# Last pair of experts: a third quarter of the down weights as whole rows, the context rows' residual through TensorE, and one fp32 pass for the last 256 columns

## The reference

```python
a = jnp.einsum('becd,edf->becf', xs, w_gate)
u = jnp.einsum('becd,edf->becf', xs, w_up)
y = jnp.einsum('becf,efd->becd', jax.nn.silu(a) * u, w_down)
y = y * gate[..., None].astype(y.dtype)
# the slots are added back to their tokens; then x = x + g2 * that
```

## Time and profile before

| | |
|---|---|
| median of 3 runs | 1518.87 us (1518.62 to 1519.34) |
| the profiled execution's own time | 1518.44 us |
| its span, first to last instruction | 1516.8 us |
| TensorE busy | 1447.9 us, 95% |
| VectorE, ScalarE busy | 623.8 us and 255.1 us |
| HBM read and written | 565.02 MB and 6.55 MB |
| mean granted TensorE clock | 0.987 of full speed |

### The profile page before, as it was taken

How to read it: one execution, slowest core, us unless ns; L and a number is a source line. 1 busy time by engine, 2 the same in 40 slices (tenths; PEclk the granted TensorE clock), 3 DMA queues, 4 the chain that set the end, 5 groups by cost and what they waited for, 6 DMA issues and landing times.

```text
span 1516.8 us, 18489 instructions
## 1 busy us (share of the span) xinstructions
PE 1447.9 (95%) x7806; PEld 883.1 (58%) x7806; DVE 623.8 (41%) x1033; ACT 255.1 (17%) x358; POOL 26.7 (2%) x58
## 2 busy tenths in 40 slices
PE   6999999999999999999999999999999889999998
PEld 3667799888899997445435335335335335335433
DVE  4454977877799996101301301301301301211313
ACT  4233223333234323000000000000000000000200
POOL 0000000000000000000000000000000000000000
PEclk8999999999999999999999999999999999999999
DMA  9999698777778759999999999999999999999999
GB/s 375 402 395 366 252 331 294 278 259 261 274 275 292 253 175 382 396 434 432 430 432 430 432 431 434 430 432 431 433 431 430 433 433 431 430 430 430 434 420 355
DMA packets 99855, 572.48 MB, mean 377 GB/s; under 512 B 9612, under 2 KB 54612, under 8 KB 76756
## 3 DMA queue, kind: packets, MB, share of 16 engines
q1 hardware_dynamic: 88416, 520.14, 84.0%
q0 software_dynamic: 6912, 50.33, 8.7%
q10 hardware_dynamic: 4468, 1.14, 0.3%
HBM read 565.02 MB, written 6.55 MB: 377 GB/s over the span
## 4 chain that ended last, share of the span: by engine, by line
PE 73%; DMA 20%; DVE 3%; SPq 2%; issue 1%; ACT 1%; DVEq 0%; ACTq 0%
PE psum L653 71%; DMA ring<-in_w_up 18%; SPq L563 2%; DMA ring<-in_w_ada 1%; DMA ring<-in_w_down 1%; SPq L450 1%; DVE w_parts L1541 1%; PE psum L663 1%; DVE ring L1689 0%; PE psum L852 0%; PE psum L1108 0%; PE psum L1078 0%; ACT w_parts L1241 0%; DVE mix L1826 0%; PE psum L815 0%
## 5 line engine op out<-in xcount | busy, mean ns | idle before, releaser
L653 PE MATMUL psum<-ring,hid 128*64 128x512 f32 x3024 | 685.9, 601 | 45.9 <-DMA ring<-in_w_up 32.6
L653 PEld LDWEIGHTS psum<-ring,hid 128*64 128x64 f32 x3024 | 243.7, 139 | 464.6 <-issue 415.5
L2004 DVE TENSOR_TENSOR hid<-psum,hid 128x512 f32<-128x512 f32 x16 | 11.1, 692 | 514.9 <-PE psum L653 514.9
L653 PE MATMUL psum<-h_parts,w_parts 128*128 128x384 f32 x1152 | 207.0, 337 | 0.0
L653 PEld LDWEIGHTS psum<-h_parts,w_parts 128*128 128x128 f32 x1152 | 199.9, 188 | 3.5 <-issue 2.5
L1541 DVE TENSOR_TENSOR w_parts<-ring,w_parts 128x2048 fp32r<-128x2048 f32 x52 | 118.9, 2287 | 48.5 <-ACT w_parts L1241 48.2
L1241 ACT ACTIVATE w_parts<-ring 128x2048 fp32r<-128x2048 f32 x52 | 99.6, 1915 | 195.3 <-PE psum L653 164.3
L653 PE MATMUL psum<-w_parts,h_parts 128*128 128x512 f32 x432 | 103.3, 395 | 0.6 <-DVE h_parts L1585 0.6
L653 PE MATMUL psum<-ring,early 128*32 128x512 f32 (+6 forms) x654 | 92.8, 538 | 7.5 <-DMA ring<-in_w_ada 6.3
L653 PEld LDWEIGHTS psum<-w_parts,h_parts 128*128 128x128 f32 x432 | 79.7, 188 | 25.6 <-issue 9.2
L653 PEld LDWEIGHTS psum<-early,mix 128*128 128x128 f32 x768 | 86.6, 192 | 9.0 <-issue 9.0
(11 more groups left out here) (223 smaller groups left out, 771.4 us busy)
## 6 DMA issues: line engine op xcount, KB each, us to landing
ring<-in_w_up SPq DMA_DIRECT2D x30, 4096.0 KB, 22.7
ring<-in_w_gate SPq DMA_DIRECT2D x28, 4096.0 KB, 29.3
ring<-in_w_down SPq DMA_DIRECT2D x26, 4096.0 KB, 29.4
ring<-in_w_ada POOLq DMA_DIRECT2D x48, 1024.0 KB, 6.9
ring<-in_w_in SPq DMA_DIRECT2D x36, 1024.0 KB, 8.3
ring<-in_w_ada SPq DMA_DIRECT2D x28, 768.0 KB, 15.6
res<-in_w_ada SPq DMA_DIRECT2D x16, 1024.0 KB, 7.0
ring<-in_w_out SPq DMA_DIRECT2D x16, 1024.0 KB, 5.7
```

Source lines behind the costliest of these rows:

```text
L653: return nc.tensor.matmul(out, lhsT, rhs, start=start, stop=stop, skip_group_check=True)
L2004: tt(by_row, bank[1][:, :].rearrange("p (b a) -> p a b", a=4), by_row, ALU.mult).then_inc(act_ready, 1)
```

## The change

Three things change, all in the last pair.

1. `FULL` goes from 2 to 3: the first two of the four rows of the second part also come as whole rows, as four loads of 1 MB in the double slot that q = 6 left. Only the last two rows come by column blocks, ten loads, all in the double slot that q = 7 left. TensorE has a third `down_full`, and each `down_tail` has half the rows. `TAIL_ORDER` has no split block.
2. The residual of the context tile is copied by ScalarE as fp32r (`kept_hi`), and VectorE makes its rest (`kept_lo`), both before the first block. `send_last` puts two passes with the identity matrix ahead of the context tile's passes, ScalarE copies the finished tile out of PSUM (`ctx_result`), and VectorE no longer adds it. VectorE also copies the identity matrix to `ident_r`.
3. The last block of 256 columns isn't split into two fp32r parts: its sending reads `y_all` in fp32. ScalarE's copy and VectorE's `y_rest` are left out for it.

```diff
-FULL = 2
+FULL = 3
-TAIL_ORDER = [("d", 0), ("h", 1), ("s", 0), ("r", 1), ("d", 2), ("s", 1), ("d", 3), ("s", 2), ("d", 4), ("s", 3), ("s", 4)]
+TAIL_ORDER = [("d", 0), ("d", 1), ("s", 0), ("d", 2), ("s", 1), ("d", 3), ("s", 2), ("d", 4), ("s", 3), ("s", 4)]
...
+        kept_hi = parts_at("kept_hi", D, res_at)
+        kept_lo = parts_at("kept_lo", D, hid_at)
+        ident_r = parts_at("ident_r", P, early_at + 4 * BANK)
...
             def full_load(n, jj, e):
-                sp.dma_start(full_rows(n, e)[:, jj, :], down_pairs(e, 0, n)[:, jj, :]).then_inc(full_landed[2 * n + jj], 16)
+                sp.dma_start(full_rows(n, e)[:, jj, :], down_pairs(e, n // 2, n % 2)[:, jj, :]).then_inc(full_landed[2 * n + jj], 16)
-            def tail_load(b, half, e):
+            def tail_load(b, e):
                 col, width = TAIL[b]
-                sp.dma_start(tail_slot(b, e)[:, 2 * half:2 * half + 2, :], down_pairs(e, 1, half)[:, :, col:col + width])\
-                    .then_inc(tail_landed[b][half], 16)
+                sp.dma_start(tail_slot(b, e), down_pairs(e, 1, 1)[:, :, col:col + width]).then_inc(tail_landed[b], 16)
...
+            sp.wait_ge(moe_used, LAST + WIDE + FULL + 1)
             for b in range(len(TAIL)):
-                sp.wait_ge(moe_used, LAST + WIDE + FULL + TAIL[b][0] // 1024 + 1)
-                for half in range(2):
-                    for e in range(2):
-                        tail_load(b, half, e)
+                for e in range(2):
+                    tail_load(b, e)
...
-                sp.wait_ge(last_out, NT * b + 1)
+                sp.wait_ge(ctx_out, b + 1)
-                sp.wait_ge(last_out, NT * (b + 1))
+                sp.wait_ge(last_out, (NT - 1) * (b + 1))
...
-            def down_tail(b, rows=range(4)):
+            def down_tail(b):
                 width = TAIL[b][1]
-                for jj in rows:
-                    if jj % 2 == 0:
-                        pe.wait_ge(tail_landed[b][jj // 2], 32)
+                pe.wait_ge(tail_landed[b], 32)
+                for jj in range(2):
...
             def send_last(b):
                 first, width = TAIL[b]
-                pe.wait_ge(y_last, b + 1)
+                cols = slice(first, first + width)
                 for t in range(NT):
                     n = NT * b + t
                     if SENDS[n] in SENDS[:n]:
-                        pe.wait_ge(last_out, n - SENDS[:n][::-1].index(SENDS[n]))
+                        old = n - 1 - SENDS[:n][::-1].index(SENDS[n])
+                        if old % NT == 0:
+                            pe.wait_ge(ctx_out, old // NT + 1)
+                        else:
+                            pe.wait_ge(last_out, (NT - 1) * (old // NT) + old % NT)
...
-                    mm(out, rows, y_hi[:, first:first + width], True, False)
-                    mm(out, rows, y_lo[:, first:first + width], False, True).then_inc(sent, 1)
+                    if t == 0:
+                        pe.wait_ge(kept_parts, 4)
+                        mm(out, ident_r[:, :], kept_hi[:, cols], True, False)
+                        mm(out, ident_r[:, :], kept_lo[:, cols], False, False)
+                    if b == len(TAIL) - 1:
+                        pe.wait_ge(tail_y, b + 1)
+                        mm(out, rows.bitcast(F32), y_all[:, cols], t > 0, True).then_inc(sent, 1)
+                    else:
+                        pe.wait_ge(y_last, b + 1)
+                        mm(out, rows, y_hi[:, cols], t > 0, False)
+                        mm(out, rows, y_lo[:, cols], False, True).then_inc(sent, 1)
...
+            for n in range(0, len(ROW_SENDS), NT):
+                cols = slice(ROW_SENDS[n][0] * BLK, (ROW_SENDS[n][0] + 1) * BLK)
+                a.wait_ge(row_added, n + 1)
+                copy(kept_hi[:, cols], y_rows[:, 0, cols]).then_inc(kept, 1)
+
+            def ctx_result(b):
+                first, width = TAIL[b]
+                a.wait_ge(sent, 16 * (PAIRS - 2) + NT * b + 1)
+                copy(y_rows[:, 0, first:first + width], bank[SENDS[NT * b]][:, 0:width]).then_inc(ctx_out, 1)
+
             for b, (first, width) in enumerate(TAIL):
-                a.wait_ge(tail_y, b + 1)
-                copy(y_hi[:, first:first + width], y_all[:, first:first + width]).then_inc(tail_hi, 1)
+                if b < len(TAIL) - 1:
+                    a.wait_ge(tail_y, b + 1)
+                    copy(y_hi[:, first:first + width], y_all[:, first:first + width]).then_inc(tail_hi, 1)
+                if b:
+                    ctx_result(b - 1)
+            ctx_result(len(TAIL) - 1)
...
             copy(actT, bank[4][:, :]).then_inc(actT_ready, 1)
+            copy(ident_r[:, :], ident[:, :])
             product(PAIRS - 1, 1, 8)
...
             add_rows(range(ROWS_LATE, len(ROW_SENDS)))
+            for n in range(0, len(ROW_SENDS), NT):
+                cols = slice(ROW_SENDS[n][0] * BLK, (ROW_SENDS[n][0] + 1) * BLK)
+                v.wait_ge(kept, n // NT + 1)
+                tt(kept_lo[:, cols], y_rows[:, 0, cols], kept_hi[:, cols].bitcast(F32), ALU.subtract).then_inc(kept_parts, 1)
...
             for b in range(len(TAIL)):
                 y_scale(b)
                 if b:
-                    result(b - 1, range(0, 1))
-                y_rest(b)
+                    result(b - 1, range(1, 2))
+                if b < len(TAIL) - 1:
+                    y_rest(b)
                 if b:
-                    result(b - 1, range(1, NT))
-            result(len(TAIL) - 1, range(NT))
+                    result(b - 1, range(2, NT))
+            result(len(TAIL) - 1, range(1, NT))
```

More of the change, by code:

```diff
@@ L163, in build @@
         ring = sb("ring", [P, RING, SLOT])
+        res_at = here()
         res = sb("res", [P, KC * T])
@@ L267, in build @@
         add_rows_of = sb("add_rows_of", [P, 33])
+        early_at = here()
         early = sb("early", [P, 32 * KC + KC * NE + P + 256])
@@ L350, in build @@
         moe_landed = [sem(f"moe_landed{n}") for n in range(WIDE)]
-        tail_landed = [[sem(f"tail_landed{n}_{half}") for half in range(2)] for n in range(len(TAIL))]
+        tail_landed = [sem(f"tail_landed{n}") for n in range(len(TAIL))]
         full_landed = [sem(f"full_landed{n}") for n in range(2 * FULL)]
@@ L384, in build @@
         tail_y, tail_hi = sem("tail_y"), sem("tail_hi")
+        kept, kept_parts, ctx_out = sem("kept"), sem("kept_parts"), sem("ctx_out")
         y_scaled, row_sent, row_added = sem("y_scaled"), sem("row_sent"), sem("row_added")
@@ L416, in tail_slot @@
             first, width = TAIL[b]
-            at = 8 * first + 4 * width * e
-            flat = ring[:, WIDE_AT[FULL + first // 1024]:WIDE_AT[FULL + first // 1024] + 2, :].rearrange("p s n -> p (s n)")
-            return flat[:, at % (2 * SLOT):at % (2 * SLOT) + 4 * width].rearrange("p (j n) -> p j n", j=4)
+            at = 4 * first + 2 * width * e
+            flat = ring[:, WIDE_AT[FULL]:WIDE_AT[FULL] + 2, :].rearrange("p s n -> p (s n)")
+            return flat[:, at:at + 2 * width].rearrange("p (j n) -> p j n", j=2)
         class Chain:
@@ L1062, in down_full @@
                                full_rows(n, e)[:, jj, col:col + width], n == 0 and jj == 0, False)
-            def down_tail(b, rows=range(4)):
+            def down_tail(b):
                 width = TAIL[b][1]
-                for jj in rows:
-                    if jj % 2 == 0:
-                        pe.wait_ge(tail_landed[b][jj // 2], 32)
+                pe.wait_ge(tail_landed[b], 32)
+                for jj in range(2):
                     for e in range(2):
                         last = mm(bank[TAIL_BANKS[b]][ES * e:ES * e + ES, 0:width], tail_rows(e, 2 * FULL + jj),
-                                  tail_slot(b, e)[:, jj, :], False, jj == 3)
+                                  tail_slot(b, e)[:, jj, :], False, jj == 1)
                 return last
@@ L1229, in _ @@
                     send_last(b)
-                elif what == "h":
-                    down_tail(b, range(0, 2))
                 else:
-                    down_tail(b, range(2, 4) if what == "r" else range(4)).then_inc(moe_used, 1)
+                    down_tail(b).then_inc(moe_used, 1)
         @block.scalar
```

## The result

The changed kernel takes 1521.63 us (median of 21 runs, 1520.46 to 1522.94) against 1519.09 us (21 runs, 1518.05 to 1520.05) of the kernel before in the same comparison: ratio 1.0016, 95% interval 1.0011 to 1.0022. That is 2.4 us slower by the ratio (2.5 by the medians), clear of noise, and within 0.2%, though the interval reaches just beyond. The forecast was 2.2 us slower: 1521.1 us, in a range of 1519.0 to 1522.9, with 0.70 for within 0.2%.

What follows compares the result with a forecast made beforehand. Loading paces the kernel up to its last weight, then TensorE's remaining work sets the end. From the last whole row at 1495.7 its terms sum to 19.9 us; the end moves 2.2 us, median 1521.1 us, range 1519.0 to 1522.9.

Steps and rivals of the forecast that it cites:

- The landings: Last pair's loads: new whole-row pairs in at 1490.7 and 1495.7, at 421 GB/s; block 1 in at 1501.1.
- TensorE unbroken behind the last whole row: Last pair: TensorE's products and sendings after 1495.7 take 19.9 us, with 0.2 us waiting, no rest from 1501.1 on.
- the sum: TensorE's steps from the last whole row at 1495.7: 19.9 us to last issue, VectorE's last result at 1516.25.
- the fp32 pass: Last 256-column block's sending: 0.43 us a tile, 1.29 for three against 0.70 for six fp32r passes, +0.59.
- the second whole row: TensorE's product with the second new row pair, for all five blocks: 3.44 us, from 1495.7 to 1499.2.
- block 4's two passes with the change of operand: Last block's sending: 0.23 us for the residual's two passes plus 0.1 for a change of kind of operand.
- The waits: TensorE before the two new whole rows: about 1.4 us (1489.3 to 1490.7) and 1.5 us.
- The rival itself: TensorE's clock falls in the new waits, if one reaches some 2.2 us: 1.7 us slower, 1522.8; chance 0.13.
- whole rows land no faster: Rival on the new loads: last whole row 0.9 us later, no faster than 2 KB pieces, 1522.0; chance 0.08.
- the extra passes are hidden: Rival on the sendings: the 1.85 + 0.59 us don't show, 1518.9 to 1520; chance 0.13.
- What it takes from VectorE: Residual in the last stretch: five VectorE results of about 0.35 to 0.68 us, said to be hidden already.
- the residual's net price: Two more TensorE passes in each of five blocks' sendings: 1.85 us on the path.

Runs made afterwards that it cites:

- rows in pieces: Changed kernel with the four new whole-row loads cut into pieces of 512 columns (2 KB); 1522.47 us against 1519.25 for the kernel before, ratio 1.0022.
- residual alone: Kernel before plus only the residual by TensorE and ScalarE; loads, order and last block unchanged; 1520.25 us against 1519.38, ratio 1.0006.
- whole rows alone: Kernel before plus only the third quarter's whole rows and their block order; 1521.31 us against 1519.38, ratio 1.0011.
- short results: Kernel before plus whole rows and their block order, context tile's results cut to 8 columns per block; 1521.36 us against 1519.25, ratio 1.0011.
- scale sooner: Kernel before plus whole rows, context results cut to 8 columns, scales of blocks 3 and 4 each ahead of one result; 1521.18 us against 1519.58, ratio 1.0011.
- sends late: Kernel before plus fp32 pass, block 1 sent before block 2's second half, blocks 2 to 4 after all products; 1519.60 us against 1519.25, ratio 1.0004.

## Why the prediction was right, point by point

**The landings.** Forecast 4.9, 9.9 and 15.3 us behind the point; measured 4.96, 9.94 and 15.37. The pace of whole rows, read from issue and landing times of two pairs of loads, held to 0.2% here (9.96 and 9.94 us) and to 1% in three other profiles (10.02 to 10.05). The working starts that landing at 1485.7 where the earlier trace rows has 1485.80, so its absolute times are 0.1 us early.

**TensorE unbroken behind the last whole row.** From there to VectorE's last result the sum gave 20.55 us; it was 1516.94 - 1496.38 = 20.56. Most terms came out within 0.02 us (2.04 and 1.87, 1.02, 1.05 and 0.43 a tile), the fp32 pass by the scaling with columns from 384. Two did not and made up for each other: the second whole row took 3.50 us, not 3.44, since it starts behind a wait, and block 4's two passes with the change of operand took 0.25 us (1514.77 to 1515.02), not 0.23 + 0.1. The mechanism held; that the sum came out to 0.01 us is in part luck. That the landings move the end was shown by the rows in pieces: 0.90 us later in, 0.90 us later out.

**Faster transfer, later end.** The whole rows did what they were meant to: the third quarter lands 0.90 us sooner than in pieces. Yet they cost 1.28 us in the changed kernel. By TensorE's sum that is because a whole row goes to all five blocks and none can be finished and sent until the last of them is in.

**The waits.** Forecast 1.4 and 1.5 from product to product; measured 1.47 and 1.48 (1.76 and 1.78 in the weight loads' rows). The granted clock stayed at 1.00. In the rows in pieces the two were 2.22 us in the weight loads' rows, and the sum above held to 0.01 us there too, so the clock cost nothing. The earlier trace rows counts by the products' rows; there the new waits are 1.31 and 1.32 us and those of the rows in pieces 1.76, so no run took this stage to the 2.20 after which the clock had fallen.

The rival itself was misread. It took 1.70 us for the longest wait without a fall and some 2.2 us for the length that decides. But the same trace has longer ones without a fall, and the changed kernel more of them (the first two rows are before, the others changed):

```profile
842.79 8.78 PE L653 MATMUL psum<-ring,hid 128*64 128x512 f32 x32 [2.53 <-DMA ring<-in_w_up]
...
1250.76 7.09 PE L653 MATMUL psum<-ring,hid 128*64 128x512 f32 x32 [2.63 <-DMA ring<-in_w_up]
843.27 8.74 PE L659 MATMUL psum<-ring,hid 128*64 128x512 f32 x32 [2.54 <-DMA ring<-in_w_up]
...
1134.70 7.09 PE L659 MATMUL psum<-ring,hid 128*64 128x512 f32 x32 [2.63 <-DMA ring<-in_w_up]
```

Of 11 such waits of 2.20 to 2.66 us, 8 were followed by slow products before and 4 in the changed kernel. A wait of this length alone doesn't say whether the clock falls.

**The rivals.** That whole rows land no faster was refuted by 421 against 387 GB/s. That the extra passes are hidden was refuted by the unbroken row of TensorE, and by residual alone (+1.05, of which 0.92 are passes).

**What was wrong in it.** One step of the residual's part: "What it takes from VectorE [...] was hidden [...] and in the last stretch it follows TensorE." That holds for the kernel before and for the changed one as it is. But it made the residual's net price 1.85 us and, by TensorE's sum, whole rows alone 1.0 us. The experiments show 0.88 and 1.86: once whole rows have pressed the blocks together, VectorE's fixed order (scale, rest, two latent results, next scale) delays the next block, unless the residual's passes make TensorE's turn longer. The two prices were off in opposite directions. The forecast wasn't touched by it, since it was summed for the changed kernel as a whole, where TensorE is unbroken. My first account of that, too much work on VectorE, fell with the short results; the order stands, by the scale sooner. It explains 0.47 us of the 0.86 between +1.0 and +1.86, measured with the context results short. The context results are 0.11 of it by the short results. The traces have about the rest: the last whole row landed 10.02 us behind the point where the sum had 9.9, and the first sending began 7.71 us behind that row (1497.13 to 1504.84 on TensorE's timeline) where the sum had 7.5 (its parts at 1503.2, the row at 1495.7). Of that, 0.14 us lie between the end of VectorE's rest and TensorE's first pass.

**What stays open.** Why the untouched part ended 0.64 us later in the changed kernel's profile. It varied by 1.75 us over the profiles, with the kernel before lowest, and the ratios of the runs agree with the differences behind the point (for sends late with that of the last store) within their intervals, wide as they are, so I take it for the spread of single executions; nothing was tried on it. The traces do show that 0.48 us of it is there by the wait at 843 us (842.79 before, 843.27 changed, rows above), long before any work that the change touches; with whole rows alone it is 1.25 of 1.31 us (844.04).

## What to carry to other kernels

A transfer that is faster in bytes can still end the kernel later: ask for each piece what may be finished once it is in, and add up the work that can't start before the last piece that everything needs. Here the total of that work after one landing, from start-to-start times, gave the end to a few hundredths of a microsecond, with single terms off by up to 0.08.

Where an engine waits in the middle of a fixed order, work placed in that wait costs next to nothing, and cutting it brings little (0.11 us for five results here); moving the instruction that another engine waits for brought 0.47. And a part that costs time by itself can cost half as much beside another that changes which engine is late, so prices of parts are measured in the company in which they are meant to run.

## What the runs showed of the hardware

Loads of 8 KB rows landed at 421 to 423 GB/s in the changed kernel, the second pair in three other profiles in 5.05 to 5.07 us, 414 to 415, and the same bytes in pieces of 2 KB at 386 to 387, with the DMA engines busy in all. Most stores at the end took 0.34 to 0.38 us to issue on SP's queue. Those that followed the one before at once took 0.42 to 0.77 us, but a few that stood alone were as slow (0.54 with whole rows alone, 0.84 with short results), so what stretches them stays open. TensorE waits of 2.19 to 2.66 us for a load were followed by a granted clock of 0.50, the level of 1.2 GHz, in some cases and not in others, within one profile (the earlier trace rows and the rows above). An fp32 product of 128 slots by 256 columns took two instructions of 0.216 us, two thirds of the 0.322 at 384 columns.
